# S5 table building in a two-block transformer kernel: chunk tables multiplied in turned form, and an earlier gather of the S5 input

## What is computed

```python
lam_bar = jnp.exp(lam * dt)
b_bar = ((lam_bar - 1.0) / lam)[..., None] * lax.complex(b_re, b_im)
bu = lax.complex(jnp.einsum('bsgp,gnp->bsgn', u, b_bar.real), jnp.einsum('bsgp,gnp->bsgn', u, b_bar.imag))
a = jnp.broadcast_to(lam_bar, bu.shape)
# combine(e1, e2) -> a1 * a2, a2 * x1 + x2
_, hs = lax.associative_scan(combine, (a, bu), axis=1, reverse=reverse)
return jnp.einsum('gpn,bsgn->bsgp', c, hs).real
```

## Time and profile before

| | us |
|---|---|
| median of 3 runs | 2929.98 (2927.48 to 2935.24) |
| the profiled execution | 2930.03 |
| its span, first to last instruction | 2928.2 |
| PE busy in the span | 2796.3 (95%) |
| DVE, ACT, POOL busy | 1570.8, 1134.6, 339.3 |

### The profile page before, as it was taken

One profiled execution on the slowest core, in us unless ns is written; L12 is line 12 of the kernel. 1 busy time (PEld: TensorE's weight loads), 2 busy tenths in 40 slices (PEclk: granted clock), 3 DMA queues, 4 the chain that ended last, 5 costly groups with the idle time before them and its releaser, 6 DMA issues. The chain is left out here.

```text
span 2928.2 us, 38710 instructions
## 1 busy us (share of the span) xinstructions
PE 2796.3 (95%) x15552; PEld 2277.3 (78%) x15552; DVE 1570.8 (54%) x2341; ACT 1134.6 (39%) x1792; POOL 339.3 (12%) x426
## 2 busy tenths in 40 slices
PE   9999999599999999999999899999999999999887
PEld 8788888488888877777788578888988888776665
DVE  7776664754434434554535654344654344664656
ACT  5332232364222324645647342223432123543443
POOL 0333221710000001111112300000000000110100
PEclk9999999799999999999999799999999999999989
DMA  4245557554444223222222323222222222211101
GB/s 142 96 147 170 156 155 222 192 160 120 130 127 116 96 75 110 70 92 80 87 94 91 126 101 101 101 88 103 69 101 89 99 100 101 82 49 40 57 15 46
DMA packets 116020, 307.08 MB, mean 105 GB/s; under 512 B 28176, under 2 KB 73808, under 8 KB 87296
## 3 DMA queue, kind: packets, MB, share of 16 engines
q1 hardware_dynamic: 108064, 278.39, 29.0%
q10 hardware_dynamic: 6336, 21.76, 2.1%
q0 software_dynamic: 1440, 4.46, 0.5%
HBM read 266.91 MB, written 41.85 MB: 105 GB/s over the span
## 5 line engine op out<-in xcount | busy, mean ns | idle before, releaser
L94 PE MATMUL ps<-hh_,wh_ 128*128 128x512 f32 x2184 | 867.2, 397 | 8.8 <-DVE hl_ L135 5.1
L94 PE MATMUL ps<-hh_,wl_ 128*128 128x512 f32 x2184 | 853.9, 391 | 0.0
L94 PE MATMUL ps<-hl_,wh_ 128*128 128x512 f32 x2184 | 853.7, 391 | 0.0
L121 DVE TENSOR_TENSOR wl_<-raw_,wh_ 128x2048 fp32r<-128x2048 f32 (+4 forms) x245 | 483.2, 1975 | 503.6 <-ACT wh_ L117 503.1
L117 ACT ACTIVATE wh_<-raw_ 128x2048 fp32r<-128x2048 f32 (+3 forms) x244 | 400.6, 1648 | 351.6 <-PE ps L94 331.2
L94 PEld LDWEIGHTS ps<-hh_,wh_ 128*128 128x128 f32 x2184 | 412.2, 189 | 107.0 <-issue 9.3
L94 PEld LDWEIGHTS ps<-hh_,wl_ 128*128 128x128 f32 x2184 | 411.9, 189 | 87.4
L94 PEld LDWEIGHTS ps<-hl_,wh_ 128*128 128x128 f32 x2184 | 412.4, 189 | 86.2 <-issue 2.9
L94 PE MATMUL ps<-ah_,wh_ 128*128 128x512 f32 x704 | 275.1, 391 | 0.0
L94 PE MATMUL ps<-al_,wh_ 128*128 128x512 f32 x704 | 274.0, 389 | 0.0
L94 PE MATMUL ps<-ah_,wl_ 128*128 128x512 f32 x704 | 274.0, 389 | 0.0
(11 more groups left out here) (363 smaller groups left out, 3584.5 us busy)
## 6 DMA issues: line engine op xcount, KB each, us to landing
raw_<-in_w SPq DMA_DIRECT2D x203, 1024.0 KB, 5.0
sO<-s5ce_ SPq DMA_DIRECT2D x32, 256.0 KB, 3.7
sW<-s5wt_ SPq DMA_DIRECT2D x16, 512.0 KB, 6.0
sA<-os_ SPq DMA_DIRECT2D x24, 256.0 KB, 2.1
ol_<-sA SPq DMA_DIRECT2D x24, 256.0 KB, 3.6
sT<-sK SPq DMA_DIRECT2D x32, 128.0 KB, 4.0
wh_<-sO ACTq DMA_DIRECT2D x4, 1024.0 KB, 6.1
wl_<-sO ACTq DMA_DIRECT2D x4, 1024.0 KB, 7.5
```

The source lines that it names most:

```text
L94: return self.e.matmul(out, lhsT, rhs, start=start, stop=stop, skip_group_check=True)
L121: return Nothing() if self.e is None else self.e.tensor_tensor(out, a, b, op)
```

## The change

**Chunk tables.** `sW` is no longer `wn` turned by PE; it is multiplied in turned form. Once, PE turns G (eight transposes, `p.gp`), ACT copies it to `s5wt`, SP stores it as `sG` in DRAM. For every packet SP loads B turned and repeated (`s5bx`, 512 KB) and, with eight DMAs of 64 KB, its part of `sG` into G (`chunk_sync`), after the packet before has finished with G (`p.f, pc - 1, 1`). DVE and POOL form `s5wt` from these two; ACT's copies and PE's transposes of each packet are gone.

**Lag products.** They need only power 0 of the old `wn`. POOL makes that `wn` (128x64 for each part) with six small operations in `scaled_b`, between its two halves of a packet; `s5fb` is a copy of the factor.

**Steps.** `steps(pc)` gives a packet 12 steps (`pc` = 0), 9 (odd) or 10 (even). `PREP_FIRST` and the number of calls of `bg()` are as before.

**Gather.** U now lies where `hl` does, free once the last up product is done. Run 0 of `spread` is issued in the FFN, at m = 3 of the last half; runs 1 and 2 after `prep_end` and the store of m = 7. DVE's fence on the tables stands behind the scaling of U, ACT's behind `rs`. DVE adds the square of m = 6 too, so the row sums are 16 products instead of 24.

**Fourier projection** (both of them): ACT makes `hh` ahead of the square, DVE adds the square of m - 1 instead of m, and the weight parts of 8 tiles are made in one piece. **GLU:** the second output tile follows two k behind the first.

```diff
@@ -376,7 +376,7 @@
...
-    if 0 < m < (6 if s in LAST else 8):
+    if 0 < m < (7 if s == 2 else 6 if s in LAST else 8):
@@ -450,20 +450,21 @@
 def project_scalar(K, ac, s, m, g, old, *bank):
+    ac.wait_ge(*K.at("x", s, m))
+    if old:
+        ac.wait_ge(*K.at(*old))
+    gained_scalar(K, ac, s, g, m)
...
-    if g is not None:
-        if old:
-            ac.wait_ge(*K.at(*old))
-        gained_scalar(K, ac, s, g, m)
 def project_vector(K, dv, s, m, g, p):
...
-    square_vector(K, dv, s, m)
-    if g is not None:
-        gained_vector(K, dv, s, g, m)
+    square_vector(K, dv, s, m - 1)
+    gained_vector(K, dv, s, g, m)
+    if m == 7:
+        square_vector(K, dv, s, m)
@@ -604,6 +605,8 @@
...
+            if f == 0 and half and m == 3:
+                spread(K, sp, 0, "U", range(8))
@@ -814,13 +818,14 @@
...
+    lows(K, dv, 8)
...
-        lows(K, dv, 4)
-        dv.bg()
-        lows(K, dv, 4)
...
+        dv.bg()
+        if m < 7:
+            lows(K, dv, 8)
@@ -931,20 +936,22 @@
...
-    for _ in range(PREP_FIRST):
-        yield
-    for pc in range(17):
+    for _ in range(PREP_FIRST + 2):
+        yield
+    sp.wait_ge(*K.at("p.gt", 1))
+    sp.dma(d["sG"].rearrange("r b q n -> q (r b) n"), P.flat.rearrange("p (b n) -> p b n", b=8)).then_inc(*K.lane("s5sG").up("p.sG"))
+    yield
+    sp.wait_ge(*K.at("p.w"))
+    sp.dma(P.bx[:, :, :], d["s5bt"][0]).then_inc(*K.lane("s5gx").up())
+    sp.wait_ge(*K.at("p.sG"))
+    chunk_sync(K, sp, 0, range(8))
+    yield
+    for pc in range(16):
...
-            un, hf = (pc - 1) // 2, (pc - 1) % 2
-            sp.wait_ge(*K.at("p.wt", pc - 1, 1))
-            sp.dma(d["sW"][un][:, 1024 * hf:1024 * hf + 1024],
-                   P.wt[:, :, :, :].rearrange("p g r x -> p (g r x)")).then_inc(*K.lane("s5sW").up("p.sW", pc - 1))
-            if pc % 4 == 0 and pc < 16:
+            yield
+            if pc % 4 == 0:
...
-        if pc == 16:
-            break
-        yield
-        yield
+            yield
@@ -952,18 +959,40 @@
...
-        yield
...
-            sp.wait_ge(*K.at("p.f", pc, 1))
+            sp.wait_ge(*K.at("p.wn", pc))
...
-        yield
+        if pc == 0:
+            yield
+            yield
+        sp.wait_ge(*K.at("p.f", pc, 1))
+        sp.dma(d["sW"][un][:, 1024 * hf:1024 * hf + 1024], P.flat).then_inc(*K.lane("s5sW").up("p.sW", pc))
+        if pc < 15:
+            sp.dma(P.bx[:, :, :], d["s5bt"][pc + 1]).then_inc(*K.lane("s5gx").up())
+        yield
+        if pc < 15:
+            chunk_sync(K, sp, pc + 1, range(4))
+        yield
+        if pc < 15:
+            chunk_sync(K, sp, pc + 1, range(4, 8))
...
-        yield
+        for _ in range(steps(pc) - (9 if pc == 0 else 7)):
+            yield
+def chunk_sync(K, sp, pc, powers):
+    for i in powers:
+        sp.dma(K.prep.G[16 * i:16 * i + 16, :, :, :].rearrange("p r s g -> p r (s g)"),
+               bass.AP(K.d["sG"].tensor, 512 * pc + 8192 * i, [[0, 16], [65536, 2], [1, 512]])).then_inc(
+            *K.lane("s5gx").up(*(("p.gx", pc) if i == 7 else ())))
@@ -998,14 +1031,8 @@
...
-        yield
-        if pc:
-            ac.wait_ge(*K.at("p.sW", pc - 1))
-        for r in range(2):
-            ac.wait_ge(*K.at("p.t", pc, r))
-            ac.act(P.wt[:, :, r, :], K.mb["p.t", pc, r].rearrange("p (g x) -> p g x", g=4), ACT.Copy).then_inc(*ac.up("p.wt", pc, r))
-            ac.mark("out", "p.t", pc, r)
-        yield
+        for _ in range(steps(pc) - 6):
+            yield
@@ -1110,17 +1140,43 @@
...
-        yield
+        for _ in range(steps(pc) - (9 if pc == 0 else 7)):
+            yield
...
-    tab, ns, cr, ci = ((P.E, 10, 2, 3), (P.G, 8, 0, 1))[x]
-    n = 4 * ns * 16
-    v = [t.rearrange("p (g s x) -> p g s x", g=4, s=ns) for t in (P.t1[:, 0:n], P.t2[:, 0:n])]
-    er, ei = (tab[:, r, :, 4 * pc:4 * pc + 4].rearrange("p s (g x) -> p g s x", x=1).broadcast_to([128, 4, ns, 16]) for r in range(2))
-    xr, xi = (P.bc[:, r, :, :].rearrange("p g (s x) -> p g s x", s=1).broadcast_to([128, 4, ns, 16]) for r in (cr, ci))
+    if x:
+        v = [t[:, 0:512].rearrange("p (g n) -> p g n", g=4) for t in (P.t1, P.t2)]
+        tabs = [t[:, r, :].rearrange("p (g n) -> p g n", g=4) for t in (P.gx, P.bx) for r in range(2)]
+        return 512, v, *tabs
+    n = 640
+    v = [t.rearrange("p (g s x) -> p g s x", g=4, s=10) for t in (P.t1[:, 0:n], P.t2[:, 0:n])]
+    er, ei = (P.E[:, r, :, 4 * pc:4 * pc + 4].rearrange("p s (g x) -> p g s x", x=1).broadcast_to([128, 4, 10, 16]) for r in range(2))
+    xr, xi = (P.bc[:, r, :, :].rearrange("p g (s x) -> p g s x", s=1).broadcast_to([128, 4, 10, 16]) for r in (2, 3))
...
+def steps(pc):
+    return 12 if pc == 0 else 10 - pc % 2
+def scaled_b(K, po, pc):
+    P = K.prep
+    t = [P.bt[:, i, :].rearrange("p (g x) -> p g x", g=4) for i in range(2)]
+    fr, fi = (P.fb[:, r, 4 * pc:4 * pc + 4].rearrange("p (g x) -> p g x", x=1).broadcast_to([128, 4, 16]) for r in range(2))
+    br, bi = P.bc[:, 0, :, :], P.bc[:, 1, :, :]
+    po.wait_ge(*K.at("p.fb"))
+    for r, (x, y, op) in enumerate(((br, bi, ALU.subtract), (bi, br, ALU.add))):
+        po.tt(t[0], x, fr, ALU.mult).then_inc(*po.up())
+        po.tt(t[1], y, fi, ALU.mult).then_inc(*po.up())
+        if r == 0 and pc:
+            po.wait_ge(*K.at("p.ab", pc - 1))
+        po.wait_ge(*po.now())
+        po.tt(P.wn[:, r, :, :], t[0], t[1], op).then_inc(*po.up(*(("p.wn", pc) if r else ())))
+        po.wait_ge(*po.now())
@@ -1164,31 +1222,32 @@
 def prep_tensor(K, pe):
...
-    for _ in range(PREP_FIRST):
-        yield
+    for _ in range(PREP_FIRST + 1):
+        yield
+    pe.wait_ge(*K.at("p.G"))
+    for r in range(2):
+        b = K.mb.take("p.gp", r)
+        pe.wait_ge(*K.after(pe, K.mb, "p.gp", r))
+        for i in range(4):
+            m = pe.tr(b[:, 128 * i:128 * i + 128], P.gx[:, r, 128 * i:128 * i + 128], K.ident)
+        m.then_inc(*pe.up("p.gp", r))
...
-        for _ in range(6):
+        for _ in range(6 - (pc == 0)):
...
-        pe.wait_ge(*K.at("p.f", pc, 1))
+        pe.wait_ge(*K.at("p.wn", pc))
...
-                pe.mm(ba[o, 0:128], wn[0:64, r, g, 7, :], ce[0:64, r, g, 0:8, :], r == 0, r == 1).then_inc(*pe.up())
-                pe.mm(bb[o, 0:128], wn[64:128, r, g, 0, :], ce[64:128, r, g, 2:10, :], r == 0, r == 1).then_inc(*pe.up())
+                pe.mm(ba[o, 0:128], wn[0:64, r, g, :], ce[0:64, r, g, 0:8, :], r == 0, r == 1).then_inc(*pe.up())
+                pe.mm(bb[o, 0:128], wn[64:128, r, g, :], ce[64:128, r, g, 2:10, :], r == 0, r == 1).then_inc(*pe.up())
...
-        yield
-        for r in range(2):
-            b = K.mb.take("p.t", pc, r)
-            pe.wait_ge(*K.after(pe, K.mb, "p.t", pc, r))
-            for g in range(4):
-                m = pe.tr(b[:, 128 * g:128 * g + 128], wn[:, r, g, :, :].rearrange("p s x -> p (s x)"), K.ident)
-            m.then_inc(*pe.up("p.t", pc, r))
-        yield
+        for _ in range(steps(pc) - 6):
+            yield
@@ -1296,11 +1355,11 @@
...
-    for n, (event, squares) in enumerate(((("ss", 2, 5), K.ssq), (("sqr", 2, 6), K.sq[0]), (("sqr", 2, 7), K.sq[1]))):
+    for n, (event, squares) in enumerate(((("ss", 2, 6), K.ssq), (("sqr", 2, 7), K.sq[1]))):
...
-                      (n, t) == (0, 0), (n, t) == (2, 7))
+                      (n, t) == (0, 0), (n, t) == (1, 7))
@@ -1383,9 +1441,13 @@
...
-    for k in range(8):
-        pe.wait_ge(*K.at("s.gl", k))
+    for at in range(10):
+        if at < 8:
+            pe.wait_ge(*K.at("s.gl", at))
...
+            k = at - 2 * m
+            if not 0 <= k < 8:
+                continue
@@ -4245,9 +4316,8 @@
...
-    for n in range(2):
-        spread(K, sp, n, "U", range(8))
...
+    spread(K, sp, 1, "U", range(8))
```

More of the change, by code:

```diff
@@ L795, in fourier_scalar @@
             ac.mark("end", "ac", f"fourier{f}")
+        ac.bg()
+        if m < 7:
+            highs(K, ac, 8)
         ac.bg()
@@ L988, in prep_scalar @@
     ac.act(u[5], u[1], ACT.Sin, scale=0.5).then_inc(*ac.up("p.s2"))
-    for _ in range(PREP_FIRST - 2):
+    for _ in range(PREP_FIRST):
         yield
+    for r in range(2):
+        ac.wait_ge(*K.at("p.gp", r))
+        ac.act(P.flat[:, 512 * r:512 * r + 512], K.mb["p.gp", r], ACT.Copy).then_inc(*ac.up("p.gt", r))
+        ac.mark("out", "p.gp", r)
     for pc in range(16):
-        for _ in range(6):
+        for _ in range(6 - 2 * (pc == 0)):
             yield
@@ L1077, in prep_vector @@
     dv.wait_ge(*K.at("p.G"))
+    dv.cp(P.fb[:, :, :], pw[:, :, 0, :]).then_inc(*dv.up("p.fb"))
     for pc in range(16):
         for x in range(2):
[L1080 removed]
+            if x and pc == 0:
+                yield
+                yield
+            out = P.ce[:, 0, :, :, :], P.wt[:, :, 0, :]
             n, v, er, ei, xr, xi = prep_views(P, pc, x)
[L1082 removed]
+            dv.wait_ge(*K.at(("p.bc", "p.gx")[x], pc))
             dv.wait_ge(*dv.now())
             dv.tt(v[0], xr, er, ALU.mult).then_inc(*dv.up())
[L1085 to L1090 removed]
+            if x:
```

(16 more changed lines are left out.)

46 lines of the change are left out of this document (22 added, 24 removed).

## The result

| | median us | runs | against the kernel before, 95% interval |
|---|---|---|---|
| before | 2929.35 | 4 | |
| after the change | 2957.95 | 4 | 1.0094 (1.008 to 1.0109) |

The change makes the kernel 28.6 us slower by the medians, 27.5 us by the ratio. The forecast was slower too, by 13 us, and its range ended at 2960; the direction holds, the size is less than half of what was measured. The profiled execution of after took 2955.59 us, its span is 2953.8, 25.6 us over that of before.

A forecast was written before the change was run, and what follows sets the result against it. PE was taken to bound the first FFN, then a serial chain to POOL's recurrence. Against 2930.0 us, -12.0 - 1.6 + 6 - 1.7 + 24.7 - 1.8 - 0.5 = +13.1 gave 2943 us, range 2930 to 2960.

The forecast's parts named there:

- Fourier to FFN: First Fourier projection: two DVE waits for the square and part of ACT's square leave the path, -1.6 us.
- the FFN from there: transposes, lag products, first packet: First FFN: transposes -12.0, three lag products moved out -1.7, first packet's stall and low clock +6 us.
- end of the down projection to the first chunk product: Tail behind the first FFN: work of packets 13 to 15 no longer hidden under PE, +24.7 us.
- from there to POOL's recurrence: First chunk product to POOL's recurrence: less low clock because PE idles 1.4 us there instead of 5.2, -1.8 us.
- GLU: Staggered output tiles in the GLU save part of the 2.1 us wait for wl_, -0.5 us.
- Packet 13 is done at about E - 0.5: End of first FFN: packet 13 done 0.5 us before the down projection ends, 8.6 us after the m = 6 x_ sum.
- Rival (c): Full queues at the end: gathers land after 10 us, U's runs late, first stall +4; 2961 us, chance 0.12.
- the two open packets: Packets 14 and 15 behind the last x_ sum: 14.0 us each with the gather as later path, 28.0 together.
- rival (b): Gather never the later path: a packet costs 11.5 us, the first packet doesn't stall; 2932 us, chance 0.20.
- The first packet: Early first FFN: packet 0's new table chain comes late, PE stalls 4 us plus some 2 of low clock, +6.
- about four steps to spare: In the FFN a packet's gather has about four steps (11 us) to spare, so repeated PE waits for DVE were excluded.
- 2948 if POOL's small products are blocked by DVE: Port lock in open packets: POOL's six small products each wait behind a DVE product, +5 us; chance 0.10.

The follow-up runs named there:

- e5_tables_late: The changed kernel with ACT's four early loads of chunk tables (1 MB each) moved behind ACT's background work; 2951.03 us, ratio 1.0071.
- e4_before_long: The kernel before with the change's packets of 12, 9 and 10 steps, tables made in the old way; 2959.38 us, ratio 1.0099.
- e11_no_gather: The changed kernel without the gather of G for packets 1 to 15, which keeps packet 0's values; 2959.1 us, ratio 1.0103.
- e6_first_later: The changed kernel with the second half of packet 0 two steps later, the packet keeping its 12 steps; 2956.85 us, ratio 1.0092.
- e7_all_three: The changed kernel with packets of 11 and 8 steps, packet 0's second half two steps later and ACT's table loads late; 2948.19 us, ratio 1.0062.
- the twelve kernels: The follow-up kernels, variants of the changed kernel or the kernel before, in three groups, each beside the kernel before; 2920.05 to 2966.09 us.
- e1_short: The changed kernel with packets of 9 (first) and 8 steps, nothing else changed; 2943.23 us, ratio 1.0038.
- e2_run0_late: The changed kernel with U's run 0 issued behind the FFN, after the store of m = 7; 2960.77 us, ratio 1.0105.

## Why the prediction was wrong

By its own terms, against the two spans:

| term | predicted | measured | from |
|---|---|---|---|
| Fourier to FFN | -1.6 | -4.2 | row sums at 100.96, before 105.20 |
| the FFN from there: transposes, lag products, first packet | -7.7 | -5.9 | 378.3 us, before 384.2 |
| end of the down projection to the first chunk product | +24.7 | +43.0 | 54.0 us, before 11.05 |
| from there to POOL's recurrence | -1.8 | +0.4 | 12.19 us, before 11.83 |
| recurrence and outputs | 0 | -0.5 | 101.9 us, before 102.4 |
| GLU | -0.5 | 0.0 | 95.0 us to the next row sums, both |
| all behind | 0 | -7.1 | -5.8 in the attention, -1.3 after |
| sum | +13.1 | +25.6 | |

**The step that failed** is "Packet 13 is done at about E - 0.5". It was done at E + 15.9, with E the end of the down projection: 16.4 us of the 18.3 that the tail was off. The `x_` sum of m = 6, from which I had counted, came at 484.74 and not at E - 9.1 = 470.1, because DVE stood ahead of it waiting for `s5bc_`; that is 14.6 us. From there on the packet took 10.4 us instead of 8.6. I had looked at SP only for the order of the issues ("16 issues, 8 to 10 us ... it has room"), never at what ACT issues at that point: the 4 MB of chunk tables filled the DMA engines just when packet 13 asked for its `s5bc_`. By e5_tables_late they are about 10 of the 16.4 us. They don't do it alone: in e4_before_long, with the same loads and packet 13 as late, DVE waits 1.12 us; SP had issued `s5bc_` 10 us sooner there. How much of the rest belongs to the U and `sT` issues on SP stays open. Rival (c) had full queues at the right size (2961) but at the wrong place: it had them delay the gathers of packets 14 and 15. Their median landing was 4.1 and 5.2 us, near the 4.5 assumed.

**Right in part by luck** are the two open packets: 28.0 predicted, 29.1 measured. I called the gather the later path (14.0 against 11.5). For packet 15 it was, at about my price: 4.9 us of issues, 4.5 of landing, 5.3 of products. But without it a packet takes 13.2 to 14.7 us (e11_no_gather), so the 11.5 was too low by 2 to 3 us, and in packet 14 the arithmetic was the later path. Had the gather landed early, as in rival (b), little would have been won. My 11.5 added durations from rows in which DVE and POOL had company of another kind; in the open POOL's product with E is 1.33 to 1.97 us, and DVE waits 1.2 to 2.0 us for POOL at three of the four parts. Even old packets take 14 us so (e4_before_long); the distance from one packet's last product to the next one's, read where DVE has nothing else to do, would have been the source to look for, and the trace of before has none.

**Smaller terms.** The first packet is 5.2 us (e6_first_later) where 6 was said, in the way foretold: DVE waits 8.07 us for `s5G_` until 140.8, PE 3.96 us at 146.8. The table came 3.7 us sooner than I had it and PE wanted the bank 3.2 us sooner, two misses that cancel. Not foreseen was PE's wait of 2.42 us for `al_` at 237.5, at the last gate product of the first half; the remark that the FFN had no such waits to fear ("about four steps to spare") counted the gather's slack and not DVE's. The low clock at 104 to 108, which I left out, did go (1.00 after), and makes the Fourier term 4.2; in e7_all_three and e11_no_gather, which have the same edit, 102 to 104 is at 0.50 again. The row sums took 7.1 us and not 5.9: the clock was 0.50 all through them, behind 45 us in which PE had little but the three lag products. It stayed at 0.50 until 538, 5 us into the chunk products, so the shorter idle time ahead of these brought none of the 1.8 us that I had put on it.

**What need not be the change.** The attention took 644.2 us in the profile of before and 638.4 in that of after. e4_before_long has the attention code of before and took 639.0; the twelve kernels lie between 638.7 and 642.4. So before's profile had a long one, and some 5 us of the -7.1 need not be a gain of the change. The medians, 28.6 us apart, are the better measure; the two profiled executions lie 0.7 us above and 2.4 us below theirs.

**Ports.** The prediction gave 2948 if POOL's small products are blocked by DVE. In after the six take 4.0 us (486.3 to 490.3) for packet 13, 3.1 for packet 14, against the 2.4 I had worked out from 0.32 each, with single ones at 0.65 to 0.71 beside DVE. So they are held up now and then, by under 2 us a packet. This agrees with the lock that the Trainium skill (SBUF — State Buffer, section SBUF: two separate sides) describes, and it is not where the loss lies.

## What to carry to other kernels

Background work that is advanced in steps has a fixed number of places: whatever a change adds to its steps comes out at the end, serial and in the open, at 14 us a packet here for work that cost nothing under PE. When the steps' place shifts, read what every queue issues at the new place, the other engines' loads included; a small load behind 4 MB of someone else's cost 10 us here, more than any instruction of the change. And time the parts of a bundle apart: here three of its four parts gain 9 us together, and the fourth, which takes 12 us off PE, loses 38 with its steps, and still 23 in the best arrangement that I tried (e1_short).

## What the runs showed of the hardware

An engine that issues DMAs can stall over it when the DMA engines are full: SP's two issues of `sO` took 7.66 us at a DMA share of 1.02 and 419 GB/s, and 1.07 us in e5_tables_late. It need not: in after eight issues of `s5G_` took 3.86 us at 479.56, with the share at 1.05 and 397 GB/s. A 128 KB load behind ACT's 4 MB landed in 6.9 us, and in 14.1 in e2_run0_late. The share alone doesn't tell how much is moved: from 460 to 465, while U and `sT` are issued, it is 1.14 at 159 GB/s. The Trainium skill (DMA: Bandwidth & Descriptors, Anatomy of one DMA) gives a fixed 2.0 us for one DMA, in a section on DMAs that GpSimd issues; those here are issued by SP, and the prediction's 2.2 us for 64 KB rested on it. The page of the profile after has 64 KB at 4.5 us in the median of 128:

```profile
s5G_<-sG SPq DMA_DIRECT2D x128, 64.0 KB, 4.5
sO<-s5ce_ SPq DMA_DIRECT2D x32, 256.0 KB, 3.1
```
